# Splitting the first expert gather of a routed layer into two halves

## The reference, cut to what matters

```python
def run(args):
    e, toks = args
    xc = t[toks]
    hid = jax.nn.silu(xc @ w_gate[e]) * (xc @ w_up[e])
    return hid @ w_down[e]
```

## Time and profile before

| | |
|---|---|
| median of 3 runs | 1001.91 us (1001.49 to 1003.04) |
| the profiled execution's own time | 1001.2 us |
| its span, first to last instruction | 999.4 us |
| TensorE busy (MATMUL records) | 976.4 us, 98% |
| TensorE weight loads | 754.0 us, 75% |
| VectorE, ScalarE, GpSimd busy | 540.9, 417.3, 52.8 us |
| chain that ended last | TensorE 85%, DMA 6%, VectorE 4% |
| DMA, mean over the span | 240 GB/s |
| expert loads, each | 1024.0 KB, median 22.4 to 25.1 us from issue to landing |

### The profile page before, as it was taken

The page is one execution under the profiler, slowest core; times in us unless marked ns, Lnnn a source line. Parts: engine busy times, 40 slices in busy tenths (PEclk is TensorE's granted clock), DMA queues, the critical chain, the costliest instruction groups (busy, mean ns, idle before and its releaser), DMA issues.

```text
span 999.4 us, 13187 instructions
## 1 busy us (share of the span) xinstructions
PE 976.4 (98%) x5289; PEld 754.0 (75%) x5289; DVE 540.9 (54%) x841; ACT 417.3 (42%) x561; POOL 52.8 (5%) x60
## 2 busy tenths in 40 slices
PE   8999999999999999999999999999999999999997
PEld 7877885653433668888888999877888878888886
DVE  5688561222332175454546595687776664545454
ACT  5565332321221063434344445575643354343442
POOL 3430000000000010000000000000210010000000
PEclk9999999999999999999999999999999999999999
DMA  8965798999999977555555646433275556556541
GB/s 289 323 237 203 302 420 330 421 421 420 421 422 420 410 227 260 182 196 174 204 172 169 220 141 226 140 114 106 88 262 177 170 180 201 188 182 195 174 162 43
DMA packets 97452, 239.59 MB, mean 240 GB/s; under 512 B 7170, under 2 KB 52314, under 8 KB 82042
## 3 DMA queue, kind: packets, MB, share of 16 engines
q1 hardware_dynamic: 95482, 229.57, 63.5%
q0 software_dynamic: 1920, 9.33, 2.7%
HBM read 237.81 MB, written 3.43 MB: 241 GB/s over the span
## 4 chain that ended last, share of the span: by engine, by line
PE 85%; DMA 6%; DVE 4%; SPq 2%; ACT 1%; issue 1%; POOL 0%; ACTq 0%; POOLq 0%; DVEq 0%
PE banks L1264 20%; PE banks L1266 20%; PE banks L1265 20%; PE banks L1618 4%; PE banks L1647 3%; DMA gain_and_spare<-in_w_down 3%; PE banks L1630 3%; DMA conv_room<-in_w_up 3%; PE banks L1321 2%; SPq L530 2%; PE banks L1611 1%; PE banks L1598 1%; PE banks L1470 1%; PE banks L1287 1%; PE banks L1742 1%
## 5 line engine op out<-in xcount | busy, mean ns | idle before, releaser
L2152 DVE TENSOR_TENSOR weights_lo<-raw_weights,weights_hi 128x2048 fp32r<-128x2048 f32 x115 | 263.3, 2290 | 142.0 <-ACT weights_hi L809 141.6
L809 ACT ACTIVATE weights_hi<-raw_weights 128x2048 fp32r<-128x2048 f32 x115 | 219.7, 1913 | 130.5 <-PE banks L1266 113.5
L1264 PE MATMUL banks<-weights_hi,normed_T_hi 128*128 128x512 f32 (+1 forms) x580 | 230.9, 398 | 0.0
L1266 PE MATMUL banks<-weights_hi,normed_T_lo 128*128 128x512 f32 (+1 forms) x580 | 224.9, 388 | 0.0
L1265 PE MATMUL banks<-weights_lo,normed_T_hi 128*128 128x512 f32 (+1 forms) x580 | 224.2, 387 | 0.0
L1264 PEld LDWEIGHTS banks<-weights_hi,normed_T_hi 128*128 128x128 f32 x580 | 109.3, 188 | 23.8 <-issue 3.0
L1266 PEld LDWEIGHTS banks<-weights_hi,normed_T_lo 128*128 128x128 f32 x580 | 108.9, 188 | 22.9
L1265 PEld LDWEIGHTS banks<-weights_lo,normed_T_hi 128*128 128x128 f32 x580 | 109.2, 188 | 19.9
L1264 PE MATMUL banks<-weights_hi,ffn_hidden_T_hi 128*128 128x512 f32 x160 | 62.4, 390 | 0.0
L1266 PE MATMUL banks<-weights_hi,ffn_hidden_T_lo 128*128 128x512 f32 x160 | 62.3, 389 | 0.0
L1265 PE MATMUL banks<-weights_lo,ffn_hidden_T_hi 128*128 128x512 f32 x160 | 62.2, 389 | 0.0
(11 more groups left out here) (425 smaller groups left out, 1701.6 us busy)
## 6 DMA issues: line engine op xcount, KB each, us to landing
raw_weights<-in_w_in SPq DMA_DIRECT2D x37, 1024.0 KB, 5.0
raw_weights<-in_ffn_w_gate SPq DMA_DIRECT2D x44, 512.0 KB, 4.0
raw_weights<-in_ffn_w_up SPq DMA_DIRECT2D x44, 512.0 KB, 5.0
raw_weights<-in_ffn_w_down SPq DMA_DIRECT2D x22, 1024.0 KB, 4.8
stage<-in_w_down SPq DMA_DIRECT2D x12, 1024.0 KB, 22.4
expert_weights<-in_w_up SPq DMA_DIRECT2D x10, 1024.0 KB, 25.1
expert_weights<-in_w_down SPq DMA_DIRECT2D x10, 1024.0 KB, 23.8
expert_weights<-in_w_gate SPq DMA_DIRECT2D x10, 1024.0 KB, 23.5
```

Source lines behind the costliest of these rows:

```text
L809: ins = eng.activation(w_hi[:, slot, :], raw, ACT.Copy)
L1264: eng.matmul(dst, x[0], w[0], start=first_one, stop=False)
L1266: return eng.matmul(dst, x[1], w[0], start=False, stop=last_one)
L2152: ins = eng.tensor_tensor(w_lo[:, slot, :], raw, w_hi[:, slot, :], ALU.subtract)
```

## The change

The gather is cut by seats instead of only by blocks. `gather(0)` makes the first 128 seats (the experts 0 to 3, all that step 0 reads) in 16 products of 128 columns, before step 0. `gather(1)` makes the other 128 (experts 4 to 7, step 1) in 16 more products of 128 columns, on TensorE's queue right behind step 0's gate and up products. ScalarE makes four copies of 512 columns instead of two of 1024; the last two stand behind step 0's silu. The seats' products are dealt 3 to step 0 and 5 to step 1 instead of 4 and 4, and 27 filling products stand before the last step instead of 30.

```diff
-BEFORE_LAST = 30
+BEFORE_LAST = 27
...
+        SEATS_AT = (0, 3, KT)
...
-            def gathered(it, kh):
+            def gathered(j, kh):
-                eng.wait_ge(ex_gath, 2 * it + (kh + 1))
-                bank = GATHER_BANK[kh]
-                eng.activation(flat(xgT[:, kh * KH:(kh + 1) * KH, :]), flat(PS[:, bank:bank + 2, :]), ACT.Copy).then_inc(ex_xT, 1)
+                eng.wait_ge(ex_gath, 2 * j + (kh + 1))
+                eng.activation(xgT[:, kh * KH:(kh + 1) * KH, P * j:P * (j + 1)],
+                               PS[:, GATHER_BANK[j] + kh, :].rearrange("p (k s) -> p k s", k=KH), ACT.Copy).then_inc(ex_xT, 1)
...
             hidden_silu(0)
-            seats_copied(range(KH))
+            for kh in range(2):
+                gathered(1, kh)
+            seats_copied(range(SEATS_AT[1]))
             rows_out(0)
             hidden_silu(1)
-            seats_copied(range(KH, KT))
+            seats_copied(range(SEATS_AT[1], KT))
...
-            def gather():
-                eng.wait_ge(sel_ready, TILES)
+            def gather(j):
                 for kh in range(2):
                     for k in range(KH):
-                        dst = PS[:, GATHER_BANK[kh] + k // 2, (k % 2) * SEQ:(k % 2 + 1) * SEQ]
+                        dst = PS[:, GATHER_BANK[j] + kh, k * P:(k + 1) * P]
                         for t in range(TILES):
-                            mm = eng.matmul(dst, tok_columns(t, kh * KH + k), sel[:, t, :],
-                                            start=(k % 2 == 0 and t == 0), stop=(k % 2 == 1 and t == TILES - 1))
+                            mm = eng.matmul(dst, tok_columns(t, kh * KH + k), sel[:, t, P * j:P * (j + 1)],
+                                            start=(k == 0 and t == 0), stop=(k == KH - 1 and t == TILES - 1))
                     mm.then_inc(ex_gath, 1)
...
                 if j >= 2:
                     eng.wait_ge(window_ready, j - 1)
                 else:
-                    eng.wait_ge(ex_xT, 1)
+                    eng.wait_ge(ex_xT, 2 * j + 1)
...
                 if j < 2:
-                    gate_then_up(experts, xgT, P * j, ex_gate, ex_gu, j == 0)
+                    gate_then_up(experts, xgT, P * j, ex_gate, ex_gu, 2 * j + 2)
...
+                if j == 0:
+                    gather(1)
                 if j < 2:
-                    gather_seats(range(KH * j, KH * (j + 1)))
+                    gather_seats(range(SEATS_AT[j], SEATS_AT[j + 1]))
...
             eng.wait_ge(tok_scaled, TILES)
-            gather()
+            eng.wait_ge(sel_ready, TILES)
+            gather(0)
```

More of the change, by code:

```diff
@@ L1620, in gate_and_up_pair, with gate_then_up @@
                 mm.then_inc(done, 1)
-            def gate_then_up(experts, rows, at, gate_done, done, by_half=False):
+            def gate_then_up(experts, rows, at, gate_done, done, xT_copied=0):
                 n = P // len(experts)
@@ L1626, in gate_then_up @@
                     for k in range(KT):
-                        if by_half and side == 0 and k == KH:
-                            eng.wait_ge(ex_xT, 2)
+                        if xT_copied and side == 0 and k == KH:
+                            eng.wait_ge(ex_xT, xT_copied)
                         for m, e in enumerate(experts):
```

## The result

The changed kernel takes 1004.8 us (median of 12 runs, 1003.67 to 1008.1) against 1002.2 us for the kernel before on the same chips (12 runs, 1001.26 to 1003.23). The ratio is 1.0028, 95% interval 1.0021 to 1.0036: slower by 2.8 us (2.1 to 3.6), where 3.5 was forecast. The profiled execution took 1004.7 us with a span of 1002.9. That is the forecast for it to the tenth, and partly by luck, as the next paragraph shows: 0.58 us of its 3.5 us came before the change could act.

What follows compares the result with a forecast made beforehand. The stream of weight loads was taken to set the experts' end. Its +3.5 us outweighs TensorE's +2.0, not added, so 1001.91 + 3.5 = 1005.4 us; range 1001.2 to 1007.2.

Steps and rivals of the forecast that it cites:

- What bounds: Experts' stretch: the stream of weight loads sets the end; it runs dry in 150 to 155 us awaiting step 0's gate.
- the hole: Weight-load stream after the change: dry from 172.8 to 176.4 us, 3.6 us, because the down loads are issued later.
- Part 1: gather(0) before step 0: 32 records at 0.24 us, 7.7 us against 7.78, so step 0 moves by -0.1 us.
- rival B: Gather's weight load cheaper without a 256-column product beside it, pace 0.17 to 0.215: 1001 to 1003.8 us; chance 0.10.
- rival A: Columns set the gather's pace, 0.111 us a record: gather(0) 3.6 us, stream and end -4.2, 997.7 us; chance 0.15.
- Parts 2 and 3: gather(1) behind step 0's up product: 7.7 us plus 0.1, uncovered; one seat moved to step 1: -1.72 and +1.72, sum nothing.
- Part 4: ScalarE's gather copies: four of 0.60 us replace two of 1.02, no gain; 0.6 us if gather(1)'s cover were gone.
- Part 5: Filling products before step 12: 1.3 us less TensorE time, no gain while the stream sets the end; adds slack.
- The stream: Weight loads: down issue 6.1 us later against 2.4 margin, hole 3.6 us, no second hole; stream moves 3.5 us.
- TensorE alone: TensorE through the experts: 7.7 us later at step 2, wins back 5.7, left +2.0, not added to the stream's +3.5.
- C: Stream keeps some backlog, so late downs open no hole of note; TensorE's +2.0 ends last: 1003.9 us; chance 0.07.

Runs made afterwards that it cites:

- Closing the hole alone: Changed kernel with all eight seat products in step 1 and none in step 0: 1003.43 us against 1001.9 for the kernel before, ratio 1.0016.
- shortening the filler alone: Changed kernel, seats still 3 and 5, with 20 filling products instead of 27: 1005.62 us against 1002.13 for the kernel before, ratio 1.0035.
- both together: Changed kernel with all eight seat products in step 1 and 20 filling products instead of 27: 1001.77 us against 1001.9 for the kernel before, ratio 1.0003.
- The adjacent layout: Changed kernel with normed rows written permuted, so gathers and router transposes read adjacent columns: 998.12 us against 1001.9 for the kernel before, ratio 0.9961.
- The 8-byte and 16-byte runs: Changed kernel, two first gathers reading columns 8 or 16 bytes apart instead of 32 (wrong rows): 999.34 and 1005.12 us against 1002.13 for the kernel before.

## Why the prediction was right, point by point

**What bounds.** The experts end on the stream of loads: shown by the chain after and by the runs in pairs. Closing the hole alone leaves TensorE last (+1.5 us by the medians), shortening the filler alone leaves the stream last, both together give 1.0003.

**Part 1.** gather(0) was forecast at 7.7 us and took 7.81; step 0's gate came 0.13 us sooner, forecast 0.1. The choice of 0.24 for the pace, out of bounds of 0.111 and 0.243, was the step on which all hung. The adjacent layout ran at the lower bound, 0.113, so both ends were real and the nearest row decided rightly. The pace of 0.24 was met (0.239); the gather is 0.1 us longer than forecast because its last record still lasts 0.40 us. Fewer columns beside the load did not make it faster to speak of, and rival B, built on that, falls. The row of the transposes, which spoke for rival A, was of another kind. Their loads in the changed kernel, 32 bytes apart, and in the one with adjacent columns:

```profile
L1290 PEld LDWEIGHTS banks<-ident,token_major x16: 185/190/207, 129.3 to 132.0; 128*128 128x128 f32 x16
...
L1290 PEld LDWEIGHTS banks<-ident,token_major x16: 138/140/142, 129.6 to 132.6; 128*128 128x128 f32 x16
```

The step costs these loads 50 ns, not 143, and eight transposes take 1.04 us in the kernel before and 1.03 with adjacent columns, so the step is not felt in their pace. Why the two kinds of load differ no run shows.

On the gather's load the trace had already sided with the Trainium skill's page SBUF — State Buffer (the note on cachelines under Door 1) against its page TensorE: Matmul & The Clock Gate (section LDWEIGHTS), whose 107 ns even the adjacent load does not meet (192 ns). The 8-byte and 16-byte runs now place the edge where that note has it in one sentence, "need ≥2 hits per line". Where the same note lets 4 fp32 be strided for free, the measurement differs if that means a step of four: 16 bytes cost 330 ns.

**Parts 2 and 3.** gather(1) took 7.89 us in the open, forecast 7.7 plus 0.1. The down issue came 5.77 us later, forecast 6.0 (6.1 relative to the shift of the gate). The seats' part was right: alone it changes nothing.

**Part 4.** The copies took 0.60 us each and nobody waited for them.

**Part 5.** Right that the shorter filler gives nothing. That it "adds slack" was half the story: in the run with 20 the slack became a wait of 3.28 us, and the granted clock fell to 0.50 behind it.

**The stream.** The hole was forecast from 172.8 to 176.4 and stands from 173.2 to 176.7 in a trace that is 0.58 us late. No second new hole opened. At the end 3.5 us were forecast, and 2.9 stand at the last load's landing, 2.8 in the time. With the gate's 0.13 and the hole's 3.5 us the stream should be 3.4 late. The stream does not make up the difference: from where traffic is back to the landing it moves 419 GB/s in both kernels (155 to 349.15 us before, 176.7 to 352.66 after). And with 30 filling products, with the same hole, the landing is 3.6 us late (210.35 against 206.73). So the 0.5 us is no larger than what one landing varies by, and no term of the sum is shown to be too large.

**TensorE alone.** Forecast +2.0, measured +1.8 where it is last.

**Rivals.** A (the columns set the pace, 997.7) is out for this layout and true for the adjacent one, at 998.1. C (no hole) is out by the stretches. The margin between the two causes was only 1.5 us, and a reader of the medians alone would have had trouble telling them apart; the pair of runs with 20 filling products did it.

## What to carry to other kernels

Before cutting a product into narrower ones, compare its pace with that of a like product whose stationary operand is adjacent: where it runs slower than its columns and the weight-load side is busy all the time, the cut doubles the cost instead of halving the wait. When the end is set by a stream of loads, list what each issue waits for and how long the stream's backlog lasts at that point; work that is added behind one trigger and ahead of the next is free up to that backlog and costs in full beyond it (here 5.9 us were added against a backlog of 2.4, and the hole was 3.5). If a layout stands in the way, pairs of float32 may already be enough.

## What the runs showed of the hardware

- A float32 load of 128 stationary columns: 192 ns adjacent, 196 at 8 bytes, 330 at 16 bytes, 335 at 32 bytes. Back to back with products of 128 columns that is 0.113, 0.119, 0.234 and 0.239 us a record. This holds for the gather's products, two records each; in the router's transposes, one record each, a load 32 bytes apart took 190 ns and an adjacent one 140.
- VectorE, 128x512 float32 products: 0.69 us in order, 0.70 in pairs 32 bytes apart, 1.16 with single floats read 32 bytes apart, 1.10 with single floats written 512 bytes apart.
- One wait of 3.28 us on TensorE, behind filling products, was followed by a granted clock of 0.50 over at least 2 us of work, and the 128 records that followed took 8.80 us instead of 7.04. The waits of 1.40 and 1.67 us near the end of the experts in the kernel before left it at 1.00.
